# A hybrid decoder layer on one core: fifteen value, key and query units as three split products in the chunk loop

## The chip, the core and the metric

The kernel runs on one NeuronCore of a Trainium2 chip. Five engines take part: TensorE (PE, matrix products into eight PSUM banks), VectorE (DVE), ScalarE (ACT), GpSimd (POOL) and SyncE (SP, which issues most of the DMAs). Each runs its own instructions in order; semaphores order them against each other. The metric is the device time in microseconds of one execution.

## The reference, cut to what matters

One decoder layer for 256 prompt tokens and 8 sequences of 4 new tokens (288 token columns), D_MODEL 2048, everything in float32:

```
h = rmsnorm(x, g_mix)
proj = h @ w_in            # q, k, v (8 heads of 128 each), indexer q and k, gates, and the RWKV-7 inputs
o_a = sparse attention     # indexer scores, causal top-k, softmax over the selected keys;
                           # the 8 sequences also see 1024 cached keys each, by a page table
o_b, state = rwkv7(...)    # decay, delta-rule state of 16 heads of 64x64, per-head norm
mixed = sigmoid(ga) * (o_a @ w_pa) + sigmoid(gb) * (o_b @ w_pb)
x = x + mixed @ w_o
x = x + (silu(h2 @ w_gate) * (h2 @ w_up)) @ w_down      # h2 = rmsnorm(x, g_ffn)
y = rmsnorm(x, g_final)
```

The outputs also hold the rotated keys, the values, the indexer keys, the RWKV states and the last normalised rows.

## The kernel before, in words

**Units and tiles.** The weights of all projections come as units of 128 output columns: 16 blocks of 128x128 float32, 1 MB. SP loads unit u into slot u % 4 of `ring` once unit u - 4 has been read (`unit_read`), in the order of the program. A unit's result is a 128x288 tile that gathers in PSUM bank u % 2; ScalarE (or VectorE) copies it out and counts `bank_free`. The numbers U_SMALL to U_DOWN name where each kind of unit begins: U_IDX (27) to 30 are the indexer queries, U_VKQ (31) to 54 the 8 value, 8 key and 8 query units, U_GA (55) on the gates.

**Plain and split products.** In a plain unit each of 16 *tiles* is one float32 matmul of a weight block in `ring` with a 288-column block of `hT`, recorded as two instructions (`tile`, L472). In the first units and from the mixing on, the products are split: ScalarE copies weights and activations to a rounded format (fp32r, "high"), VectorE subtracts to get the "low" rest, and three products (high*high, low*high, high*low) stand for one float32 product (L504 to L506, L1032 to L1034, L1077 to L1079).

**Filling.** `fill` puts plain tiles into TensorE's program wherever other work leaves gaps. `vkq(t0, t1)` does it for value, key and query tiles counted from 32 on: `vkq(-32, ...)` starts with tile 0, so `vkq(6, 10)` is tiles 38 to 41. These places are written out by hand:

- The decay chain (about 195 to 285 us): the low-rank products (L585), then norms (L594, L602), bonus products (L617), nine gram products (L628, one for each chunk and one for the samples), with VectorE's long elementwise passes between. Here TensorE does the indexer units and the first value tiles.
- The sample part (285 to 364 us): self scores (L739), cached indexer scores (`scores`), the sample steps and the prompt's indexer scores. VectorE inverts the gram triangles (from L1793) and starts the top-k.
- The chunk loop (`chunk`, 364 to 563 us): 8 chunks of 32 tokens of the RWKV state. A chunk has four groups of small matmuls (transposes L794 and L796, x L812 and L816, u L825, outputs and state L834 to L842) with 6, 8, 7, 6 and 7 plain tiles ahead of, between and behind them: 34 tiles a chunk, 272 in all, after 112 that came earlier. ScalarE evicts after each group (`turned`: eight pieces behind the transposes) and stages the next chunk; VectorE evicts the other halves, multiplies the state, rotates the keys and queries that are complete (`rotate`) and goes on with the top-k (`largest`).
- Behind the loop: the value rows are turned (L854 to L860), then prompt attention and the cached scores (`kscore`, L929 to L939) alternate. Sequence 0's key pages (`first_keys`, 8 pages of 512 KB into KP[0]) are loaded during the loop. When `chunk_done` says that the loop is over and they have landed, SP reads the page numbers of sequence 1 (`keys_of`, L388) and issues its 16 half pages (`k_half`, L395).

**SP's order** around the gram stage: units up to U_VKQ + 3; then, after `dve_stage` 4, eight pages of indexer keys; for every chunk a gram store and one page; eight pages; unit U_VKQ + 4; eight pages; unit U_VKQ + 5; after `sidx`, sixteen pages; then the rest. GpSimd only issues DMAs between its first squares and the end.

`arena` is one SBUF area of 35520 columns whose parts serve several tensors in turn; `area(at, ...)` names a float32 view, `over(...)` one in fp32r.

Of the kernel before, what the change touches and what calls it, by code (L numbers as in the profile page):

```python
# [20 lines left out]
P = 128  # L21
# [26 lines left out]
U_DOWN = U_FF + 2 * FT  # L48
U_END = U_DOWN + 4 * KT

# [69 lines left out]
def program(nc, wst, wdn, xT, cst_d, prm_d, lora_d, kT_d, v_d, ki_d, wkv_d, pt_d, o_y, o_k, o_v, o_ki, o_wkv,  # L120
            o_shift, o_wkvs):
    with ExitStack() as ctx:
# [64 lines left out]
        UPD = [area(at, 2, NB * DB) for at in (9472, 15104, 1540, 28160)]  # L187
# [78 lines left out]
        def over(name, base, at, shape, dt=F32R):  # L266
# [15 lines left out]
                        over("first_h_lo", "arena", 7168 + KT * NX, [P, KT, NX]))  # L282
        x1_d = nc.dram_tensor("residual", (P, KT, NT), F32)
# [30 lines left out]
        def _(sp):  # L314
# [61 lines left out]
            units(U_VKQ + 5, U_VKQ + 6, unit)  # L376
# [21 lines left out]
            units(U_VKQ + 6, U_GA + 1, unit)  # L398
# [3 lines left out]
            first_keys(4, NPG)  # L402
# [9 lines left out]
            sp.wait_ge(sem("chunk_done"), NCH + 1)  # L412
            sp.wait_ge(sem("k_in0"), 16 * NPG)
# [42 lines left out]
        def _(pe):  # L456
# [132 lines left out]
            pe.wait_ge(sem("h_done"), 1)  # L589
            pe.wait_ge(sem("dve_stage"), 1)  # L590
            pe.wait_ge(sem("lora_out"), 2 * CT)
# [4 lines left out]
            fill(U_IDX, 6, 20)  # L596
# [7 lines left out]
            fill(U_IDX, 20, 42)  # L604
# [7 lines left out]
            for j in range(CT):  # L612
                if j == 4:
                    fill(U_IDX, 42, 4 * KT)
# [4 lines left out]
            vkq(-32, -17)  # L619
# [12 lines left out]

            vkq(-8, 2)
# [99 lines left out]
            vkq(2, 6)  # L733
# [8 lines left out]
            vkq(6, 10)  # L742
# [6 lines left out]
            vkq(10, 12)  # L749
            scores_sum(0)  # L750
            pe.wait_ge(sem("states_in"), 16)
            for j in range(CT):
                if j == 4:
                    sample_step(0)
                state_term(j)
                vkq(12 + 2 * j, 14 + 2 * j)
# [4 lines left out]
            vkq(28, 31)  # L761
            sample_step(1)
            vkq(31, 37)
            sample_step(2)
            for n in range(3, 7):
                vkq(25 + 4 * n, 29 + 4 * n)
# [5 lines left out]
            vkq(53, 58)  # L772
            sample_step(7)
            vkq(58, 62)
            sample_step(8)
            vkq(62, 66)
            sample_step(9)
            pe.wait_ge(sem("scs_out"), 2)
            for n in range(2 * IH):
                prompt_scores(n)  # L780
                if n % 2 == 1 and n < 14:
                    vkq(65 + n, 67 + n)
                if n == 5:
                    sample_step(10)
            at_tile = 112

            def chunk(n, at):

                fill(U_VKQ, at, at + 6)
# [9 lines left out]
                fill(U_VKQ, at + 6, at + 14)  # L799
# [19 lines left out]
                fill(U_VKQ, at + 14, at + 21)  # L819
# [8 lines left out]
                fill(U_VKQ, at + 21, at + 27)  # L828
# [16 lines left out]
                fill(U_VKQ, at + 27, at + 34)  # L845

            pe.wait_ge(sem("sample_act"), 63)
            for n in range(NCH):
                chunk(n, at_tile + 34 * n)
# [94 lines left out]
            for n in range(2 * HA + 3):  # L944
# [7 lines left out]
                if n == 7:  # L952
                    pe.wait_ge(sem("var_out"), CT)
                if n >= 7:
                    fill(U_GA, 11 * (n - 7), min(11 * (n - 6), 8 * KT))
# [182 lines left out]
        def _(act):  # L1138
# [75 lines left out]
            act.wait_ge(sem("index_rows"), 3)  # L1214
            ch(fn(SG, SG, ACT.Sigmoid))
# [4 lines left out]
            act.wait_ge(sem("lora_out"), 2 * CT)  # L1220
            act.wait_ge(sem("norm_out"), CT + 2)
# [25 lines left out]
            evict(-2 + 32)  # L1247
# [97 lines left out]
            evict(8 + 32)  # L1345
# [13 lines left out]
            evict(28 + 32)  # L1359
# [5 lines left out]
            evict(37 + 32)  # L1365
            sample_step(2)
            for n in range(3, 7):
                evict(29 + 4 * n + 32)
# [8 lines left out]
            evict(58 + 32)  # L1377
            sample_step(7)
            evict(62 + 32)
            sample_step(8)  # L1380
            evict(66 + 32)
            sample_step(9)
            for n in range(2 * IH):
                prompt_relu(n)
                evict(min(67 + n, 80) + 32)
                if n == 5:
                    sample_step(10)
            at_tile = 112
# [12 lines left out]
            def chunk(n, at):  # L1401
# [10 lines left out]
                evict(at + 14)  # L1412
                act.wait_ge(sem("x_done"), n + 1)
                fn(XS[0:CH], ps[2][0:CH, :].rearrange("p (h i) -> p h i", i=64), ACT.Copy).then_inc(sem("x_out"), 1)
                evict(at + 21)
# [4 lines left out]
                evict(at + 27)  # L1420
# [5 lines left out]
                evict(at + 34)  # L1426
# [4 lines left out]
            for n in range(NCH):  # L1431
                chunk(n, at_tile + 34 * n)
            act.wait_ge(sem("vrows"), 1)
            for t in range(2):
# [167 lines left out]
        def _(dve):  # L1602
# [273 lines left out]

            for n in range(NCH):
                chunk(n)
            rotate(HA - 1)
# [233 lines left out]
        def _(pool):  # L2113
# [30 lines left out]
            pool.wait_ge(sem("states_done"), 4)  # L2144
            pool.dma_start(o_wkvs, SST).then_inc(sem("wkvs_out"), 16)
# [101 lines left out]
```

## Time and profile before

| | us |
|---|---|
| median of 3 runs (range) | 1982.94 (1981.04 to 1983.49) |
| the profiled execution | 1981.97 |
| its span | 1979.7 |
| TensorE matmuls busy | 1938.5 (98%) |
| VectorE busy | 1024.7 (52%) |
| ScalarE busy | 729.1 (37%) |
| GpSimd busy | 38.2 (2%) |

The profile shows one execution. "Busy" leaves out waits, and matmuls overlap, so a busy TensorE need not be at its peak. In the lists below a group is: engine, line, operation, output <- input, count; times are in us from the start of the span. "Granted clock" (PEclk) is the share of TensorE's full clock that the chip allowed: 1.00 is 2.4 GHz, 0.50 is 1.2 GHz.

### The profile page before, as it was taken

To read this page: it belongs to the slowest core of one execution; us is meant where nothing else is said; L and a number is where in the kernel's file an instruction comes from. 1 tells how busy PE (TensorE), PEld (TensorE's weight loads), DVE (VectorE), ACT (ScalarE), POOL (GpSimd) and SP (SyncE) were. 2 spreads that over 40 slices of the span, in tenths; PEclk is the share of its full clock that TensorE was granted. 3 is DMA by queue.
4 is the path that set the end of the run, shared out by engine and by line. 5 is a ranking of instruction groups with operands and counts; after the bars stand their busy time and mean duration, and the time that the engine had idled before them with its cause. 6 is when DMAs were issued, how large, how long until landed. Compare 5 with 4: busy or idle time off the path is not lost.

```text
span 1979.7 us, 37998 instructions
## 1 busy us (share of the span) xinstructions
PE 1938.5 (98%) x15641; PEld 1769.2 (89%) x15641; DVE 1024.7 (52%) x1256; ACT 729.1 (37%) x963; POOL 38.2 (2%) x55
## 2 busy tenths in 40 slices
PE   8999999999989999999999999999999999999997
PEld 7999666688866766899999999999999999999997
DVE  6655849677644510455545545555544554444443
ACT  5333204422223110444444444444444444333332
POOL 0000011000000000000000000000000000000000
PEclk9999999999999999999999999999999999999999
DMA  6454284445567999544455544444444444544443
GB/s 262 167 174 170 99 239 130 138 131 189 186 250 265 345 380 403 201 164 170 170 209 183 192 168 160 163 168 170 169 160 162 166 170 150 209 161 162 168 166 121
DMA packets 105431, 376.35 MB, mean 190 GB/s; under 512 B 28898, under 2 KB 38754, under 8 KB 78210
## 3 DMA queue, kind: packets, MB, share of 16 engines
q1 hardware_dynamic: 78514, 344.13, 48.8%
q0 software_dynamic: 4576, 18.92, 2.8%
q10 hardware_dynamic: 22256, 12.13, 2.2%
q8 instruction: 58, 0.95, 0.2%
q14 instruction: 27, 0.22, 0.0%
HBM read 357.53 MB, written 17.58 MB: 189 GB/s over the span
## 4 chain that ended last, share of the span: by engine, by line
PE 93%; DVE 2%; SPq 2%; DMA 1%; ACT 1%; issue 1%; POOLq 0%; ACTq 0%; DVEq 0%
PE ps L472 16%; PE ps L1077 14%; PE ps L1078 14%; PE ps L1079 14%; PE ps L1032 5%; PE ps L1033 5%; PE ps L1034 5%; PE ps L505 3%; PE ps L504 3%; PE ps L506 3%; PE ps L988 1%; PE ps L939 1%; PE ps L516 1%; SPq L395 1%; DMA arena<-in_kT 1%
## 5 line engine op out<-in xcount | busy, mean ns | idle before, releaser
L2038 DVE TENSOR_TENSOR weights_lo<-ring,weights_hi 128x2048 fp32r<-128x2048 f32 (+1 forms) x152 | 305.7, 2011 | 284.9 <-ACT weights_hi L1546 284.9
L1078 PE MATMUL ps<-h_lo,weights_hi 128*128 128x288 f32 x1408 | 416.1, 296 | 0.0
L1077 PE MATMUL ps<-h_hi,weights_hi 128*128 128x288 f32 x1408 | 414.6, 294 | 0.4 <-DVE weights_lo L2038 0.4
L1079 PE MATMUL ps<-h_hi,weights_lo 128*128 128x288 f32 x1408 | 412.5, 293 | 0.0
L1546 ACT ACTIVATE weights_hi<-ring 128x2048 fp32r<-128x2048 f32 (+1 forms) x152 | 257.1, 1692 | 367.4 <-PE ps L1079 358.4
L472 PE MATMUL ps<-hT,ring 128*128 128x288 f32 x1408 | 368.4, 413 | 0.0
L472 PEld LDWEIGHTS ps<-hT,ring 128*128 128x128 f32 x1408 | 260.5, 191 | 77.8 <-issue 10.3
L1079 PEld LDWEIGHTS ps<-h_hi,weights_lo 128*128 128x128 f32 x1408 | 265.1, 188 | 0.0
L1077 PEld LDWEIGHTS ps<-h_hi,weights_hi 128*128 128x128 f32 x1408 | 264.1, 188 | 0.7 <-DVE weights_lo L2038 0.7
L1078 PEld LDWEIGHTS ps<-h_lo,weights_hi 128*128 128x128 f32 x1408 | 264.4, 188 | 0.1
L1077 PE MATMUL ps<-act_hi,weights_hi 128*128 128x288 f32 x704 | 208.4, 296 | 0.0
L1078 PE MATMUL ps<-act_lo,weights_hi 128*128 128x288 f32 x704 | 207.7, 295 | 0.0
L1079 PE MATMUL ps<-act_hi,weights_lo 128*128 128x288 f32 x704 | 207.0, 294 | 0.0
L1966 DVE TENSOR_TENSOR weights_lo<-ring,mix_weights_hi 128x2048 fp32r<-128x2048 f32 x48 | 110.0, 2292 | 90.2 <-ACT mix_weights_hi L1495 90.2
L1495 ACT ACTIVATE mix_weights_hi<-ring 128x2048 fp32r<-128x2048 f32 x48 | 91.8, 1913 | 119.0 <-PE ps L1034 119.0
L1079 PEld LDWEIGHTS ps<-act_hi,weights_lo 128*128 128x128 f32 x704 | 132.6, 188 | 0.0
L1078 PEld LDWEIGHTS ps<-act_lo,weights_hi 128*128 128x128 f32 x704 | 132.2, 188 | 0.0
L1077 PEld LDWEIGHTS ps<-act_hi,weights_hi 128*128 128x128 f32 x704 | 131.9, 187 | 0.0
L505 PE MATMUL ps<-first_h_lo,first_weights_hi 128*128 128x296 f32 x384 | 115.2, 300 | 0.0
L506 PE MATMUL ps<-first_h_hi,weights_lo 128*128 128x296 f32 x384 | 114.6, 299 | 0.0
L504 PE MATMUL ps<-first_h_hi,first_weights_hi 128*128 128x296 f32 x384 | 114.6, 298 | 0.0
L1145 ACT ACTIVATE first_weights_hi<-ring 128x2048 fp32r<-128x2048 f32 x27 | 51.7, 1915 | 93.7 <-PE ps L506 88.6
(369 smaller groups left out, 2876.4 us busy)
## 6 DMA issues: line engine op xcount, KB each, us to landing
ring<-in_wst SPq DMA_DIRECT2D x207, 1024.0 KB, 4.9
ring<-in_wdn SPq DMA_DIRECT2D x64, 704.0 KB, 4.0
arena<-in_v SPq DMA_DIRECT2D x64, 512.0 KB, 6.0
arena<-in_kT SPq DMA_DIRECT2D x112, 256.0 KB, 5.4
arena<-chunk_ar_bk ACTq DMA_DIRECT2D x24, 256.0 KB, 3.7
arena<-in_ki SPq DMA_DIRECT2D x64, 64.0 KB, 2.7
arena<-in_kT SPq DMA_DIRECT2D x8, 512.0 KB, 6.2
arena<-in_xT SPq DMA_DIRECT2D x4, 592.0 KB, 6.6
```

The costliest lines, as they stand in the source:

```text
L472: ins = mm(out, ring[:, slot, k, :], rhs(k), start=(k == 0), stop=(k == KT - 1))
L504: mm(out, W_HI1[:, (u0 + s) % 2, w], H_HI1[:, k, :], start=(k == 0), stop=False)
L505: mm(out, W_HI1[:, (u0 + s) % 2, w], H_LO1[:, k, :], start=False, stop=False)
L506: ins = mm(out, W_LO[:, slot, w], H_HI1[:, k, :], start=False, stop=(k == KT - 1))
L1032: mm(out, MW_HI[:, (u - U_MIX) % 2, w], hi, start=start, stop=False)
L1033: mm(out, MW_HI[:, (u - U_MIX) % 2, w], lo, start=False, stop=False)
L1077: mm(out, W_HI[:, (u - U_FF) % 2, w], hi, start=start, stop=False)
L1078: mm(out, W_HI[:, (u - U_FF) % 2, w], lo, start=False, stop=False)
L1079: return mm(out, W_LO[:, u % 4, w], hi, start=False, stop=stop)
L1546: fn(W_HI[:, (u - U_FF) % 2, 0:n], ring[:, u % 4].rearrange("p k c -> p (k c)")[:, 0:n], ACT.Copy).then_inc(sem("w_high"), 1)
L1966: tt(W_LO[:, u % 4], raw, MW_HI[:, (u - U_MIX) % 2].bitcast(F32), ALU.subtract).then_inc(sem("mix_w_split"), 1)
L2038: tt(W_LO[:, u % 4, 0:m], raw, W_HI[:, at, 0:m].bitcast(F32), ALU.subtract).then_inc(sem("w_split"), 1)
```

## The change

- 137 plain tiles now come before the loop instead of 112. The 25 more stand in the decay chain: `fill(U_IDX, 6, 10)` ahead of L594, 30 tiles instead of 22 ahead of L617, 19 instead of 15 ahead of the grams, two instead of one behind each gram. All later `vkq` calls are shifted by 25. In ScalarE's program the sigmoid of SG (L1215) moves behind the 16 low-rank sigmoids. SP loads unit U_VKQ + 6 ahead of the wait on `sidx`.
- Units U_VKQ + 9 to U_VKQ + 23 (15 units, the last seven key units and the eight queries) are done in the loop as split products: 720 of them, in halves of 24 (`key_products`), 94 a chunk (64 in chunk 0, 92 in chunk 7), divided over the five places of a chunk by `loop_part`. Seven plain tiles stand at the loop's start.
- ScalarE copies the high part of each half (1024 columns) into one of two buffers (`key_weights_high`), inside its chunk program at the places where it evicted units (`progress`), and before the loop the high part of h into four free pieces of SBUF.
- GpSimd subtracts the low part of each half in place in `ring`. The store of the sample states moves behind its 19th half.
- VectorE makes the low part of h in place of `hT` before the loop, and adds high and low again after it; TensorE's gate tiles wait for that.
- The free pieces lie where sequence 0's key pages 5 to 7 went: SP loads these only after the loop and after h is restored. UPD's second area moves.

```diff
+U_SPLIT, N_SPLIT = U_VKQ + 9, 15
+N_PLAIN = 137
+def loop_part(n, s):
+    part = lambda m: 0 if m < 0 else min(48 * N_SPLIT, (64 + 94 * (m // 5 - 1) + (17, 39, 58, 75, 94)[m % 5])
+                                          if m >= 5 else (0, 17, 33, 48, 64)[m])
+    return part(5 * n + s - 1), part(5 * n + s)
+def high_free(q):
+    return 0 if q < 2 else 24 if q == 2 else 24 * (q - 2) + 16
...
-            units(U_VKQ + 5, U_VKQ + 6, unit)
+            units(U_VKQ + 5, U_VKQ + 7, unit)
             sp.wait_ge(sem("sidx"), 1)
...
-            first_keys(4, NPG)
+            first_keys(4, 5)
...
             sp.wait_ge(sem("chunk_done"), NCH + 1)
+            sp.wait_ge(sem("first_h_split"), 5 * 4 + 8)
+            first_keys(5, NPG)
             sp.wait_ge(sem("k_in0"), 16 * NPG)
...
-            pe.wait_ge(sem("dve_stage"), 1)
             pe.wait_ge(sem("lora_out"), 2 * CT)
+            fill(U_IDX, 6, 10)
+            pe.wait_ge(sem("dve_stage"), 1)
...
-                vkq(-17 + c, -16 + c)
-            vkq(-8, 2)
+                vkq(-1 + 2 * c, 1 + 2 * c)
+            vkq(17, 27)
...
-            vkq(6, 10)
+            vkq(31, 35)
             scores(0)
...
+            def key_products(p0, p1):
+                for p in range(p0, p1):
+                    q, k, part = p // 24, p // 24 % 2 * 8 + p % 8, p % 24 // 8
+                    u = U_SPLIT + p // 48
+                    if p % 48 == 0:
+                        pe.wait_ge(sem("bank_free"), u + 1)
+                    kind = ("hh", "lh", "hl")[part] if q == 0 else ("hh", "hl", "lh")[part]
+                    if p % 24 == 0:
+                        pe.wait_ge(sem("first_high"), U_IDX + q + 1)
+                    if p == 0:
+                        pe.wait_ge(sem("first_h_high"), 5 * 4 + 4)
+                    if kind == "lh" and p % 8 == 0:
+                        pe.wait_ge(sem("first_split"), U_IDX + q + 1)
+                    if kind == "hl" and p < 48 and p % 8 == 0:
+                        pe.wait_ge(sem("first_h_split"), 5 * 4 + 4)
+                    ...
+                    if kind == "hl" and p % 8 == 7:
+                        ins.then_inc(sem("key_high_read"), 1)
...
+            def key_weights_high():
+                q = key_high[0]
+                u = U_SPLIT + q // 2
+                act.wait_ge(sem(f"w_in{u % 4}"), 16 * (u // 4 + 1))
+                if q >= 2:
+                    act.wait_ge(sem("key_high_read"), q - 1)
+                    act.wait_ge(sem("first_split"), U_IDX + q - 1)
+                fn(VW_HI[q % 2], ..., ACT.Copy).then_inc(sem("first_high"), 1)
+            def progress(to):
+                while key_high[0] < 2 * N_SPLIT and high_free(key_high[0]) <= to:
+                    if 48 * (evicted[0] - 8) <= high_free(key_high[0]):
+                        evict(KT * (evicted[0] + 1))
+                    else:
+                        key_weights_high()
+                while 48 * (evicted[0] - 8) <= to and evicted[0] < 3 * HA:
+                    evict(KT * (evicted[0] + 1))
+            act.wait_ge(sem("pidx_sum"), 2 * IH)
+            act.wait_ge(sem("wkv_out"), 16)
+            key_weights_high()
+            key_weights_high()
+            for a, b, high in V_HI:
+                fn(high[:, :, :], hT[:, a:b, 0:NT], ACT.Copy).then_inc(sem("first_h_high"), 1)
             act.wait_ge(sem("inv_stored"), 32 * NCH)
             stage_inverse(0)
             values(0)
...
+            dve.wait_ge(sem("unit_read"), U_SPLIT)
+            for g, (a, b, high) in enumerate(V_HI):
+                dve.wait_ge(sem("first_h_high"), 5 * 4 + g + 1)
+                tt(H_LO[:, a:b, 0:NT], hT[:, a:b, 0:NT], high[:, :, :].bitcast(F32), ALU.subtract)...
             for n in range(NCH):
                 chunk(n)
+            dve.wait_ge(sem("unit_read"), U_GA)
+            for a, b, high in V_HI:
+                tt(hT[:, a:b, 0:NT], H_LO[:, a:b, 0:NT].bitcast(F32), high[:, :, :].bitcast(F32), ALU.add)...
             rotate(HA - 1)
...
+            for q in range(2 * N_SPLIT):
+                u, at = U_SPLIT + q // 2, q % 2 * KT * P // 2
+                pool.wait_ge(sem("first_high"), U_IDX + q + 1)
+                nc.gpsimd.tensor_tensor(W_LO[:, u % 4, w], ring[...][:, w], VW_HI[q % 2].bitcast(F32),
+                                        ALU.subtract).then_inc(sem("first_split"), 1)
```

## Rows read from the trace of the kernel before

**Rows 1.** Windows: us, then busy us (count) of each engine, granted clock, DMA.

```profile
400.00:500.00 100.00, 100.00 (x1108) 80.64 (x1108) 77.54 (x116) 26.57 (x61) 0.60 (x1) 1.00 0.48 160
...
1300.00:1400.00 100.00, 100.00 (x760) 100.00 (x760) 50.60 (x48) 45.36 (x40) 0.00 (x0) 1.00 0.47 166
```

**Rows 2.** Table of waits, TensorE: us in total, times, longest.

```profile
PE ps L617 <- DVE arena L1713: 2.8, 1, 2.8
PE ps L628 <- DVE arena L1756: 2.2, 1, 2.2
```

**Rows 3.** Chain of waits, chunks 1 and 2: start, us, what.

```profile
410.45 6.50 PE ps L472 x26
...
435.27 6.50 PE ps L472 x26
```

**Rows 4.** Window of the decay chain behind the wait of L617.

```profile
232.00:236.00 4.00, 4.00 (x11) 2.79 (x10) 3.62 (x12) 0.00 (x0) 0.00 (x0) 0.57 0.00 0
```

**Rows 5.** Instructions in order of time, TensorE: start, us, instructions, [idle before <- releaser].

```profile
231.70 3.50 PE L617 MATMUL ps<-arena,cst 128*128 128x288 f32 x8 [2.80 <-DVE arena L1713]
...
246.10 2.10 PE L617 MATMUL ps<-arena,cst 128*128 128x288 f32 x8
```

**Rows 6.** Instructions in order of time, TensorE at the self scores.

```profile
285.10 0.42 PE L739 MATMUL ps<-arena 128*32 128x4 f32 x16 [0.82 <-ACT arena L1251]
```

**Rows 7.** Instructions in order of time, SP's queue behind the gram stores.

```profile
276.23 9.28 SPq L359 DMA_DIRECT2D arena<-in_ki  x9
285.55 0.44 SPq L316 DMA_DIRECT2D ring<-in_wst  x1
```

**Rows 8.** Line 316 between 284 and 287 us, issue to landing.

```profile
DMA to landing us min/median/max: 7.6/7.6/7.6
```

**Rows 9.** Instructions in order of time at the loop's entry, and wide passes.

```profile
212.29 2.12 ACT L1223 ACTIVATE arena<-arena 128x2304 f32<-128x2304 f32 x1
...
364.15 3.18 PE L472 MATMUL ps<-hT,ring 128*128 128x288 f32 x12
...
364.66 1.07 DVE L1787 SCALAR_TENSOR_TENSOR arena<-arena,small 128x256 f32<-128x256 f32 x2 [0.73 <-ACT arena L1245]
...
365.21 1.15 ACT L1318 ACTIVATE arena<-arena 128x512 f32<-128x512 f32 x2 [0.30 <-issue]
...
366.31 2.50 DVE L1844 TENSOR_TENSOR arena<-arena,prm 128x2304 f32<-128x2304 f32 x1
```

**Rows 10.** Instructions in order of time, ScalarE behind the transposes of chunk 2.

```profile
418.74 1.57 ACT L1397 ACTIVATE arena<-ps 32x256 f32<-32x256 f32 x4 [6.19 <-PE ps L796]
...
421.95 1.15 ACT L1318 ACTIVATE arena<-arena 128x512 f32<-128x512 f32 x2
```

**Rows 11.** Instructions in order of time, GpSimd and VectorE at the start.

```profile
5.29 4.17 POOL L2117 TENSOR_TENSOR arena<-arena 128x1152 f32<-128x1152 f32 x2 [4.83 <-DMA arena<-in_xT]
...
7.35 3.71 DVE L1632 SCALAR_TENSOR_TENSOR first_h_lo<-arena,prm,first_h_hi 128x288 fp32r<-128x288 f32 x4 [5.38 <-ACT first_h_hi L1154]
...
15.11 1.79 DVE L1632 SCALAR_TENSOR_TENSOR first_h_lo<-arena,prm,first_h_hi 128x288 fp32r<-128x288 f32 x4
```

**Rows 12.** Instructions in order of time, SP and TensorE around the loop's end.

```profile
528.13 3.62 SPq L383 DMA_DIRECT2D arena<-in_kT  x4
...
558.22 1.13 PE L842 MATMUL ps<-arena 64*64 64x64 f32 x32
...
562.78 1.04 PE L854 MATMUL ps<-cst,arena 128*128 128x128 f32 x8
...
564.15 12.14 SPq L395 DMA_DIRECT2D arena<-in_kT  x16
...
583.69 5.35 PE L939 MATMUL ps<-arena 128*32 128x256 f32 x64 [2.54 <-DMA arena<-in_kT]
```

**Rows 13.** Line 383 (key pages of 512 KB), issue to landing.

```profile
DMA to landing us min/median/max: 5.9/6.2/6.6
```

**Rows 14.** The page's GB/s of DMA in 40 slices of 49.5 us.

```profile
GB/s 262 167 174 170 99 239 130 138 131 189 186 250 265 345 380 403 201 164 170 170 209 183 192 168 160 163 168 170 169 160 162 166 170 150 209 161 162 168 166 121
```

More of the change, by code:

```diff
@@ L396, in k_half @@
                         "a p n -> p (a n)")[:, w]).then_inc(sem(f"k_in{half}"), 16)
-            units(U_VKQ + 6, U_GA + 1, unit)
+            units(U_VKQ + 7, U_GA + 1, unit)
             sp.wait_ge(sem("wkvs_out"), 16)
@@ L595, in _ @@
             ins.then_inc(sem("norm"), 1)
-            fill(U_IDX, 6, 20)
+            fill(U_IDX, 10, 24)
             pe.wait_ge(sem("norm_out"), CT + 3)
@@ L603, in _ @@
                    tile_position=(g, 0)).then_inc(sem("norm"), 1)
-            fill(U_IDX, 20, 42)
+            fill(U_IDX, 24, 54)
             def vkq(t0, t1):
@@ L613, in _ @@
                 if j == 4:
-                    fill(U_IDX, 42, 4 * KT)
+                    fill(U_IDX, 54, 4 * KT)
+                    vkq(-32, -20)
                 if j >= 4:
@@ L781, in _, with chunk @@
                 if n % 2 == 1 and n < 14:
-                    vkq(65 + n, 67 + n)
+                    vkq(90 + n, 92 + n)
                 if n == 5:
                     sample_step(10)
-            at_tile = 112
-            def chunk(n, at):
-                fill(U_VKQ, at, at + 6)
+            def key_products(p0, p1):
[13 more added lines that the diff above has]
+                        pe.wait_ge(sem("first_h_split"), 5 * 4 + 4)
+                    k0, high = [(a, t) for a, b, t in V_HI if a <= k < b][0]
+                    w = (W_LO[:, u % 4, k * P:(k + 1) * P] if kind == "lh" else VW_HI[q % 2][:, k % 8 * P:(k % 8 + 1) * P])
+                    h = H_LO[:, k, 0:NT] if kind == "hl" else high[:, k - k0, :]
+                    ins = mm(ps[u % 2][:, 0:NT], w, h, start=(p % 48 == 0), stop=(p % 48 == 47))
+                    if kind == "hl" and p % 8 == 7:
+                        ins.then_inc(sem("key_high_read"), 1)
+                    if p % 48 == 47:
+                        ins.then_inc(sem("unit_read"), 1)
+            def chunk(n):
+                if n == 0:
+                    fill(U_VKQ, N_PLAIN, 9 * KT)
+                key_products(*loop_part(n, 0))
                 pe.wait_ge(sem("sbk_in"), 32 * (n + 1))
@@ L798, in chunk @@
                 ins.then_inc(sem("turned"), 1)
-                fill(U_VKQ, at + 6, at + 14)
+                key_products(*loop_part(n, 1))
                 pe.wait_ge(sem("sgr_in"), 16 * (n + 1))
@@ L818, in chunk @@
                 ins.then_inc(sem("x_done"), 1)
-                fill(U_VKQ, at + 14, at + 21)
+                key_products(*loop_part(n, 2))
                 pe.wait_ge(sem("sti_in"), 32 * (n + 1))
@@ L827, in chunk @@
                 ins.then_inc(sem("u_done"), 1)
-                fill(U_VKQ, at + 21, at + 27)
+                key_products(*loop_part(n, 3))
                 pe.wait_ge(sem("u_out"), 2 * n + 2)
@@ L844, in chunk @@
                 ins.then_inc(sem("chunk_done"), 1)
-                fill(U_VKQ, at + 27, at + 34)
+                key_products(*loop_part(n, 4))
             pe.wait_ge(sem("sample_act"), 63)
             for n in range(NCH):
-                chunk(n, at_tile + 34 * n)
+                chunk(n)
             pe.wait_ge(sem("state"), NCH + 1)
@@ L1399, in turned, with chunk @@
                        ACT.Copy).then_inc(sem("turned_out"), 1)
-            def chunk(n, at):
+            def chunk(n):
                 if n == 1:
```

81 lines of the change are left out of this document (50 added, 31 removed).

## The prediction

> **What bounds the kernel now.** I read the windows of 100 us first: between 400 and 500 us, inside the chunk loop, TensorE is busy all the time while VectorE stands at 77.5 and ScalarE at 26.6 us [rows 1]. The table of waits then shows that TensorE idles in few places: in the decay chain (2.8 us ahead of the blk products of L617, 2.2 us ahead of the gram products of L628) [rows 2]. So little is lost anywhere else: a plain tile taken out of the loop is worth its full time, and a tile put into the decay chain costs only what the idle time there does not swallow. Last I read the queues and the other engines in order of time around four places: the gram stage, the loop's entry, the inside of a chunk, the loop's end. The change adds a wait or moves a transfer at each of them.
>
> The sum is made against the profiled execution's own 1981.97 us (span 1979.7); the median of the runs is 1982.94, 1.0 us more. A measurement here can tell about 0.2%, 4.0 us, from no change.
>
> **1. Split products for plain tiles (gain).** The 13 plain tiles between two chunks' matmuls, recorded as 26, take 6.50 us, and a chunk lasts 24.8 us [rows 3]; a tile is 0.500 us and a chunk's 34 tiles are 17.0. A split product of the same shape runs in the FFN at 760 per 100 us [rows 1], 0.132 us. Chunks 1 to 6 each issue 94 of them (12.4 us), chunk 7 issues 92 (12.1), chunk 0 issues 7 plain tiles and 64 products (11.9). That is 6 x 4.6 + 4.9 + 5.1 = 37.8 us less. The 7.8 us of scan matmuls per chunk stay.
>
> **2. 25 tiles into the decay chain.** They are 12.5 us of work: 4 ahead of the norms, 8 ahead of L617, 4 ahead of the grams, 9 among them. They replace the 2.8 and 2.2 us of idle time and some 4 us of shorter waits. Behind the 2.8 us the granted clock was 0.57 on average, with 1.2 GHz in part of the stretch [rows 4], and the same eight products took 3.50 us instead of 2.10 [rows 5]; a long wait costs some 1.7 us beyond itself, and two such are covered here. VectorE's chain starts 1.2 us later because four tiles now stand ahead of the norm matmuls; moving the SG sigmoid gives 0.7 back. Followed wait by wait, the self scores (L739, at 285.10) [rows 6] come 0.8 us later: **+0.8**, between -1 and +3.
>
> **3. Unit 35 is wanted before it is loaded.** PE now does tile 64 of the value and key units (the first of unit U_VKQ + 4) right behind L739; before, it was at tile 38 there. SP loads that unit in an unchanged place: behind the last gram store and nine index-key pages that take 9.28 us, so at 285.55, and it landed 7.6 us later [rows 7, 8]. The grams' end moves it by 0.5 us, to a landing at 293.6. PE comes from L739 at 286.3, does one tile and waits from 286.8: 6.8 us, and 1.7 for the clock, **+8.5** (5 to 9: less if it lands sooner or the clock stays up). Behind PE wait the cached scores and, through ScalarE's in-order queue, the odd gram loads of VectorE's inverse, so nothing downstream takes it back.
>
> **4. Entry of the loop.** TensorE's last prompt score before the fill ended at 364.15 [rows 9]. It then does 7 plain tiles, 3.5 us, to 367.7, and needs `sv_done` for the transposes (chunk 0 has no split product ahead of them). ScalarE must first wait for VectorE's last prompt sum (365.7), then copy two halves of weights and the whole of h, 6656 columns. By 2.12 us for 2304 columns that is 6.6 us with the fixed parts of six instructions, to 372.4; then two DMA issues and the value copies (1.15 us) end at 374.5 [rows 9]. Idle time 6.8 us, +1.7 clock: **+8.5** (6 to 10). GpSimd's two low halves and VectorE's low part of h (5.4 us) end before product 16 needs them.
>
> **5. High parts inside a chunk.** ScalarE makes the high part of half q only after product 24q - 32, and stands in its own order: after the transposes it evicts for 3.2 us and copies values for 1.15 [rows 10], then copies the half (1.0 us), 5.4 us after the transposes. Half 8 (freed at product 160, two products into chunk 2) is wanted at product 192, 17 products or 2.2 us behind the transposes; half 12 in chunk 3 after 19, half 16 in chunk 4 after 21. TensorE waits 3.2, 3.0 and 2.7 us, each with 1.7 of clock: **+14.0** (9 to 16; below, if the clock stays up). The other halves are freed early enough.
>
> **6. Evictions against a shorter part.** The x matmuls need ScalarE's evictions, 3.2 us after the transposes [rows 10]. The 8 tiles between hid them; 17 products (2.2 us) in chunk 0 and 22 (2.9 us) later don't: 1.1 + 4 x 0.4 = **+2.7** (chunks 2 to 4 are already waiting).
>
> **7. GpSimd's subtraction.** The trace has GpSimd on 1152 columns in 2.1 us [rows 11], none with this output. For 1024 columns I take 1.9 to 2.3; below is no gain, since only a late one is seen. A half is consumed every 5 us, so up to 3.5 us costs at most 1.5, and 4.2 us (twice the row) 6. I take 0.
>
> **8. Behind the loop.** VectorE restores h in four passes, 5.4 us by 2.50 for 2304 columns [rows 9], ahead of the last rotation. SP loads pages 5 to 7 only then: issues 0.9 us apart (3.62 for four), landing in 6.2 [rows 12, 13], so the last is in 14.0 us after the last value, key and query product. Only then does SP read the next page numbers (4.8 us: from the last chunk's end at 559.3 to the first issue at 564.15) and start sequence 1's 16 half loads. Before, these started 1.4 us after that product (564.15 against 562.8), and the matmuls on them at 583.69 [rows 12], 20.9 us after it. Now: 14.0 + 4.8 + 3.5 MB ahead of the first half's end and 1 MB of g2, 4.5 MB at the 403 GB/s of the densest slice [rows 14], 11.2, + 2 to land = 32.0. **+11.2** (7 to 15); both versions have the slow clock there. The extra idle time of sequence 0's scores lies inside it.
>
> Sum: -37.8 + 0.8 + 8.5 + 8.5 + 14.0 + 2.7 + 0 + 11.2 = **+7.9 us**: 1989.9 on the profiled basis, 1991 on the runs' median.
>
> **The shared port, by row and by page.** While GpSimd squared x (5.29 to 9.46), four scaled subtractions of VectorE took 3.71 us instead of 1.79 [rows 11]: VectorE stood still, GpSimd did not slow. The Trainium skill ("SBUF — State Buffer", "Who interferes with whom") says that a VectorE instruction with two SBUF inputs and a GpSimd instruction that reads SBUF exclude each other for the whole instruction; the trace agrees. By that rule each of the 30 low halves can hold VectorE or be held: where no such meeting lies on the path the sum stays 1991, with one in each chunk it is the last rival's time.
>
> **Rivals.**
> - *Not the forecast's stalls but ScalarE in time* (faster). If the copies of halves 8, 12 and 16 end within 2.2 us of the transposes, step 5 is gone: 1991 - 14 = 1977. For it: ScalarE is busy only 26.6% [rows 1]. Against: what counts is its order, and 4.35 us of other work stands ahead. Chance 0.17.
> - *The load of unit 35 hides* (no change): 1991 - 8.5 = 1982.5. It decides at a landing before 287. For it: only the queue's order makes it late. Against: DMA queues were full then. 0.18.
> - *The key pages hide*: if the loads behind the loop overlap what PE waits for anyway, step 8 falls by 11 to 1980. Against: sequence 1's scores already waited 2.5 us before the change [rows 12]. 0.10.
> - *VectorE becomes the bound.* Its work in a chunk is 0.775 x 24.8 = 19.2 us on average [rows 1, 3], against 20.2 for TensorE's new chunk. One block of 2.1 us per chunk on the path makes 7 x 2.1 = 15 us: 2006. It decides once VectorE loses over 1 us a chunk. Against: the waits of steps 5 and 6 give it room. 0.08.
> - The forecast, all steps within their bounds, 1984 to 1999: 0.47.
>
> The range takes in the bounds of the steps and reaches to the first rival: 1977 to 1999. Slower by over 0.2% (above 1986.9): most of the forecast, the fourth rival and a little of the second, 0.57. Within 0.2%: the second and third mostly, 0.25. Faster (below 1979): 0.18.
>
> **What would show it.** Step 1: the loop's products at 0.132 us each. Step 2: no wait over 1 us before L739. Step 3: TensorE idle some 7 us behind L739, ended by a DMA into ring. Step 4: 7 us idle ahead of the first transposes, ended by ScalarE. Step 5: three waits near 3 us on ScalarE's high parts in chunks 2, 3 and 4, none in 5 to 7. Step 8: sequence 1's scores 32 us after the last query product. Wrong would be: a chunk near 20.5 us throughout, or waits on GpSimd's low parts in most chunks.

## The result, and the profile after

The changed kernel takes 2005.18 us (median of 4 runs, 2000.17 to 2008.33) against 1981.99 us before: ratio 1.0114, 95% interval 1.0091 to 1.0136, so 23.2 us slower. The forecast was 1991 (1977 to 1999): the sign came out, the size was about three times too small (+7.9 us in the sum), and the time lies outside the range. The profiled run took 2005.82 us, with a span of 2004.0: 24.3 us more than before.

TensorE's table of waits in the changed kernel (us in total, times, longest):

```profile
PE ps L988 <- DMA arena<-in_kT: 11.8, 3, 6.9
PE ps L828 <- ACT key_weights_hi_a L1449: 8.9, 3, 3.2
...
PE ps L493 <- DMA ring<-in_wst: 6.6, 1, 6.6
PE ps L919 <- DVE arena L1913: 5.7, 1, 5.7
PE ps L843 <- ACT arena L1369: 5.4, 1, 5.4
PE ps L861 <- ACT arena L1477: 3.0, 5, 0.8
```

The waits of [rows 2] are gone, and those of steps 3, 4, 5, 6 and 8 stand in their place. In order of time on TensorE and SyncE's queue (start, us, instructions, idle time before):

```profile
285.48 0.42 PE L762 MATMUL ps<-arena 128*32 128x4 f32 x16 [0.30 <-ACT arena L1302]
293.20 3.25 PE L493 MATMUL ps<-hT,ring 128*128 128x288 f32 x6 [6.62 <-DMA ring<-in_wst]
...
374.04 3.66 PE L493 MATMUL ps<-hT,ring 128*128 128x288 f32 x14
383.07 1.94 PE L843 MATMUL ps<-cst,arena 128*128 128x128 f32 x8 [5.37 <-ACT arena L1369]
...
428.48 1.23 PE L828 MATMUL ps<-h_lo,key_weights_hi_b 128*128 128x288 f32 x8
429.54 0.43 PE L828 MATMUL ps<-key_h_hi_b,weights_lo 128*128 128x288 f32 x2
...
433.99 0.64 PE L828 MATMUL ps<-key_h_hi_a,key_weights_hi_a 128*128 128x288 f32 x3 [3.24 <-ACT key_weights_hi_a L1449]
...
569.56 1.03 PE L903 MATMUL ps<-cst,arena 128*128 128x128 f32 x8
575.72 2.51 SPq L402 DMA_DIRECT2D arena<-in_kT  x3
586.60 6.53 PE L988 MATMUL ps<-arena 128*32 128x256 f32 x64 [4.63 <-DMA arena<-in_kT]
591.13 9.55 SPq L414 DMA_DIRECT2D arena<-in_kT  x16
608.06 6.04 PE L988 MATMUL ps<-arena 128*32 128x256 f32 x64 [6.95 <-DMA arena<-in_kT]
```

The self scores (285.10 in [rows 6]) start at 285.48. The fill ahead of the loop (364.15 in [rows 9]) starts at 374.04, 9.9 us later. The loop, from that fill to the value rows' transposes (562.78 in [rows 12], 569.56 here), takes 195.5 us instead of 198.6. From there to sequence 1's scores it is 38.5 us instead of 20.9: +17.6. What comes later is as long as before (1395.94 and 1396.01 us). So 9.9 - 3.1 + 17.6 - 0.1 = 24.3 us: all of the loss has a place.

Windows of the same run; the last column but two is the granted clock. The first row is chunk 2, the second chunk 5, the third lies behind the loop; the last is the kernel before, behind its loop:

```profile
426.59:453.92 27.33, 24.09 (x305) 22.89 (x303) 19.83 (x31) 10.56 (x19) 9.70 (x4) 0.88 0.36 116
507.73:529.26 21.53, 20.97 (x304) 20.00 (x303) 17.49 (x25) 10.35 (x19) 9.78 (x5) 1.00 0.53 168
...
576.00:590.00 14.00, 6.79 (x58) 3.20 (x62) 4.23 (x10) 0.83 (x3) 0.00 (x0) 0.50 0.57 198
```
```profile
564.00:582.00 18.00, 13.96 (x151) 9.00 (x148) 11.02 (x28) 5.69 (x16) 1.61 (x3) 1.00 0.91 337
```

A chunk with no wait but one of 0.56 us lasts 21.4 to 21.5 us, down from 24.8 [rows 3]. A chunk with a 3.24 us wait lasts 27.3, and the clock was at 1.2 instead of 2.4 GHz in a quarter of it. Behind the loop it was at 1.2 GHz throughout 576 to 590. In the kernel before it was not: 1.00 from 564 to 582, and 0.72 in the 6 us after that.

### The profile page after: what moved, and what is told of

Read it like the earlier page. It is cut to its first block, busy times and chain, and to the rows that moved or that the text cites. A ratio compares the mean times of both kernels' runs of the same rounds, so it can differ in the third digit from the quotient of the medians.

```text
span 2004.0 us, 38581 instructions
## 1 busy us (share of the span) xinstructions
PE 1933.3 (96%) x15881; PEld 1786.5 (89%) x15881; DVE 1049.1 (52%) x1264; ACT 763.0 (38%) x997; POOL 112.9 (6%) x85
## 4 chain that ended last, share of the span: by engine, by line
PE 91%; ACT 2%; DMA 2%; SPq 2%; DVE 1%; issue 1%; ACTq 0%; DVEq 0%
PE ps L1128 14%; PE ps L1129 14%; PE ps L1130 14%; PE ps L493 10%; PE ps L1083 5%; PE ps L1085 5%; PE ps L1084 5%; PE ps L828 4%; PE ps L526 3%; PE ps L525 3%; PE ps L527 3%; PE ps L1039 1%; DMA arena<-in_kT 1%; PE ps L988 1%; PE ps L537 1%
## 5 line engine op out<-in xcount | busy, mean ns | idle before, releaser
L493 PE MATMUL ps<-hT,ring 128*128 128x288 f32 x928 | 246.0, 416 | 8.0 <-DMA ring<-in_wst 6.6
L493 PEld LDWEIGHTS ps<-hT,ring 128*128 128x128 f32 x928 | 172.6, 192 | 62.6 <-issue 11.8
```

Of the source, the lines that this page charges most:

```text
L493: ins = mm(out, ring[:, slot, k, :], rhs(k), start=(k == 0), stop=(k == KT - 1))
```

## The experiments

My theory was that the loss is a sum of separate waits, each with a stretch of lower clock behind it. The main rival was the prediction's last: GpSimd's subtractions hold VectorE on the shared port, and VectorE becomes the bound of the loop. Medians below stand against the changed kernel's 2005.2 us, which was timed on its own; the ratios are to the kernel before, timed on the same chip beside each experiment (1980.5 to 1982.1 us), so a difference of 2 us between medians says nothing.

**e1_load**: unit 35's load ahead of eight key pages.

```
+            units(U_VKQ + 4, U_VKQ + 5, unit)
             ki_pages(2, 0, 8)
-            units(U_VKQ + 4, U_VKQ + 5, unit)
```

> The changed kernel (2005.2 us) with one edit on SyncE: the load of unit U_VKQ + 4 is issued ahead of the eight index-key pages of pair 2 instead of behind them. Theory (the loss is a sum of added waits, each with a stretch of lower clock behind it): the 6.6 us wait of the plain tiles at 293 us goes, and with it the 10.2 us at the lower clock that cost some 2.9; the loop's fill starts at 364.5 instead of 374.0 and the time is 1996, between 1994 and 1998. Rival (the waits in front of the loop are not what sets the end: VectorE's inverse and the gram loads would have held the loop back anyway): the wait goes, another ahead of the loop takes its place, and the time stays above 2003.

Measured: 2002.6 us (1997.5 to 2007.6), ratio 1.0091 [1.0057, 1.0125]. A miss: the time fell between the theory's and the rival's. The load was issued at 274.81 instead of 285.46, but TensorE still waited 5.2 us for it. Its one landing time, and what the DMA engines did meanwhile (second last column their busy share, last column GB/s; the next experiment's expectation says 120 GB/s, these rows say 350 and 203):

```profile
DMA to landing us min/median/max: 14.8/14.8/14.8
```
```profile
276.00:282.00 6.00, 6.00 (x28) 4.53 (x27) 5.90 (x4) 0.00 (x0) 5.30 (x8) 1.00 1.02 350
282.00:288.00 6.00, 2.14 (x23) 1.14 (x21) 0.87 (x3) 2.44 (x7) 0.57 (x1) 0.93 0.98 203
```

SyncE's order is only a part of what makes the load late: the DMA engines are full from 276 to 288 us, and the load issued into them took 14.8 us to land. What it gained was lost again behind it. TensorE went on 3.55 us earlier than in the changed kernel (289.65 against 293.20) and was 3.5 us later at 352.60 (349.07). Between them ScalarE's seven gram loads took 9.00 us to issue instead of 4.59, its next eviction came late, and TensorE waited and then had the lower clock. The first row is the changed kernel's, the others are e1_load's:

```profile
299.55 4.59 ACTq L1403 DMA_DIRECT2D arena<-gram  x7
```
```profile
295.52 9.00 ACTq L1403 DMA_DIRECT2D arena<-gram  x7
308.31 1.92 PE L687 MATMUL ps<-arena,small 64*32 64x512 f32 x4 [1.57 <-ACT arena L1391]
```
```profile
308.00:320.00 12.00, 11.69 (x84) 7.68 (x84) 10.74 (x36) 1.77 (x5) 0.00 (x0) 0.50 0.59 186
```

This is the rival's picture, in one profiled run, the second slowest of six.

**e1b_load**: the same load ahead of the gram stores (`units(U_VKQ + 4, U_VKQ + 5, unit)` above `for c in range(NCH):`).

> In e1_load the load was issued 10.7 us earlier (274.8 instead of 285.5) and landed only some 3.5 us earlier, 14.9 us after its issue, beside the gram stores' short packets (DMA engines busy all the time at 120 GB/s). Here the load of unit U_VKQ + 4 is issued ahead of the first gram store, near 263. Theory (what made unit 35 late is the DMA engines' queue in the gram stage, of which the issue's place is only a part): it lands before 283, no wait over 0.5 us for the ring before 300, no lower clock at 289, and the fill ahead of the loop starts 8 to 10 us earlier than in the changed kernel (374.0); time 1996, between 1992 and 1999. Rival (the data behind the grams, index keys and gram loads, are late themselves): the 5 to 7 us of idle time appear at the cached scores or the states instead, and the time stays above 2001.

Measured: 2000.6 us (1998.5 to 2003.8), 1.0093 [1.0069, 1.0118]. The wait for the ring is gone, and another stands at the grams: VectorE waits for a gram store behind the MB, and TensorE for VectorE. The time fell by 4.6 us and lies between the theory's range and the rival's mark, as in e1_load.

```profile
263.76 0.44 SPq L335 DMA_DIRECT2D ring<-in_wst  x1
270.59 1.51 DVE L1837 TENSOR_TENSOR arena<-ps,cst 128x512 f32<-128x512 f32 x2 [8.91 <-DMA gram<-arena]
271.34 1.97 PE L651 MATMUL ps<-arena 64*64 64x64 f32 x32 [4.73 <-DVE arena L1837]
```

**e7_load_first**: the load earlier still, behind unit 34 and ahead of SyncE's wait for the B and K rows (`units(22, U_VKQ + 5, unit)`).

> The changed kernel with the load of unit U_VKQ + 4 issued ahead of SyncE's wait for the B and K rows, so ahead of the index-key pages of pair 1 too, near 250 us, when its slot of the ring is free. e1_load and e1b_load turned the wait of 6.6 us into waits of 5.2 us for the same load and of 4.7 us for the gram stage. Theory (from 253 us the DMA engines are full, and a MB put in anywhere among them is paid for by someone; before that they have room): no wait over 1 us for the ring or for the gram stage, the fill ahead of the loop starts at 365 instead of 374, time 1996, between 1993 and 1999. Rival (the engines have no room at 250 either): another wait of 4 us or more between 250 and 300, time above 2000.

Measured: 1991.9 us (1989.1 to 1995.8), 1.0042 [1.0018, 1.0066]: 13.3 us less, more than expected (1993 to 1999). Issued at 248.15 it landed in 4.8 us, in a place where the changed kernel's DMA engines are busy only a quarter of the time (this row is the changed kernel's), and no wait replaced it (rows of e7_load_first):

```profile
250.00:254.00 4.00, 4.00 (x18) 3.13 (x17) 3.73 (x10) 0.40 (x1) 0.77 (x1) 1.00 0.26 100
```
```profile
283.73 0.42 PE L761 MATMUL ps<-arena 128*32 128x4 f32 x16 [0.34 <-ACT arena L1301]
284.08 2.21 PE L492 MATMUL ps<-hT,ring 128*128 128x288 f32 x8
```

The first transposes of the loop start at 371.79. In the changed kernel they start at 383.07, and in e2_high, e3_keys, e5_zero_low and e10_tail, whose programs are the same up to there, at 380.87 to 383.86. So the load was worth 9.1 to 12.1 us there, and some 2 us of the gain can be the spread between runs.

**e2_high**: ScalarE copies freed high halves before it waits for the transposes.

```
+                progress(loop_part(n, 0)[1])
                 act.wait_ge(sem("turned"), n + 1)
```

> The changed kernel with one line more on ScalarE: in each chunk the high halves that the products ahead of the transposes have freed are copied before ScalarE waits for the transposes. Theory (waits and the clock behind them): the three waits on high halves (3.2, 3.0, 2.7 us) fall below 0.5 us each, the three stretches of 6.8 us at the lower clock in chunks 2, 3 and 4 go too (3.4 us each), and the time falls by 17 to 19 us to 1987, between 1984 and 1990. Rival (VectorE, held by GpSimd's subtractions on the port that both use, is the bound of a chunk): the three waits turn into waits on VectorE's copies or state, and the time stays above 2002.

Measured: 1992.7 us (1990.7 to 1998.8), 1.0046 [1.0024, 1.0068]: -12.5 us, short of 17 to 19 and outside the range (1984 to 1990). The three waits are gone. Chunks 2 and 4 of e2_high, and the long wait left in chunk 4:

```profile
427.08:448.48 21.40, 20.84 (x304) 19.97 (x303) 19.82 (x30) 10.56 (x19) 10.11 (x5) 1.00 0.47 159
469.90:494.91 25.01, 22.44 (x305) 21.45 (x304) 24.29 (x33) 10.34 (x19) 10.96 (x5) 0.93 0.62 211
```
```profile
482.10 1.39 PE L874 MATMUL ps<-arena 32*32 32x64 f32 x32 [2.00 <-DVE arena L1936]
```

Chunks 2 and 3 fell from 27.3 and 27.1 to 21.4 us; in chunk 4 (26.7 before) VectorE, busy 24.3 of 25.0 us, now comes last at the u matmuls, 2.0 us plus the clock. It is late because it meets GpSimd twice just before, in the two instructions of its last update of the sample states (rows of e2_high):

```profile
467.50 3.42 DVE L1920 TENSOR_TENSOR arena<-arena 128x1024 f32<-128x1024 f32 x1
470.95 3.29 DVE L1921 TENSOR_TENSOR arena<-arena,small 128x1024 f32<-128x1024 f32 x1
```
```profile
467.23 2.60 POOL L2239 TENSOR_TENSOR weights_lo<-ring,key_weights_hi_b 128x1024 fp32r<-128x1024 f32 x1 [5.74 <-ACT key_weights_hi_b L1449]
469.82 3.33 POOL L2239 TENSOR_TENSOR weights_lo<-ring,key_weights_hi_a 128x1024 fp32r<-128x1024 f32 x1
```

The same two VectorE instructions take 1.22 and 1.23 us in the update before (446.10), which begins between two subtractions (GpSimd's next one starts at 448.14), and 1.22 each in e5_zero_low, where GpSimd reads nothing: 4.3 us less for the pair. So the rival has its place, but in one chunk of eight, and there it costs 3.6 us (25.01 against 21.40). That the 2.0 us wait would go with GpSimd's reads is inferred; no run took them out of e2_high.

**e5_zero_low**: GpSimd writes zeros and reads nothing (`nc.gpsimd.memset(W_LO..., 0.0)`), so the weights' low parts are left out.

> The changed kernel with GpSimd writing zeros instead of the low parts of the 15 split units: the weights' low parts are left out of the result; GpSimd no longer reads SBUF for them, every signal and every product stays. Theory (waits on ScalarE and SyncE, with the clock): none of the waits goes, VectorE's instructions in the loop get shorter (no L1961 of 3.1 us, no L1951 of 2.1 us), and the time falls by 0 to 2 us: 2004, between 2002 and 2006. Rival (the shared port makes VectorE the bound of the loop): the loop gets at least 1 us a chunk shorter, 1996 or less.

Measured: 2002.6 us (1996.8 to 2006.2), 1.0091 [1.0056, 1.0126]. Two undisturbed chunks of the changed kernel, and then two of e5_zero_low:

```profile
507.73:550.66 42.93, 41.82 (x606) 39.97 (x605) 37.54 (x52) 20.66 (x38) 19.25 (x9) 1.00 0.63 208
```
```profile
502.27:545.13 42.86, 41.74 (x607) 39.99 (x606) 34.90 (x55) 20.65 (x38) 7.62 (x8) 1.00 0.62 201
```

VectorE's busy time falls by 2.6 us and GpSimd's by 11.6, the two chunks' by 0.07. The rival falls for the undisturbed chunks, and for those alone; chunk 4 of e2_high is the other case. The 2.6 us between the medians is inside the spread of both.

**e3_keys**: behind the loop, sequence 0's pages on a semaphore of their own; no wait for their landing.

```
             sp.wait_ge(sem("chunk_done"), NCH + 1)
+            pages = keys_of(1)
             sp.wait_ge(sem("first_h_split"), 5 * 4 + 8)
             first_keys(5, NPG)
-            sp.wait_ge(sem("k_in0"), 16 * NPG)
-            pages = keys_of(1)
```

> The changed kernel with SyncE's order behind the loop changed: sequence 0's pages count on a semaphore of their own, sequence 1's page numbers are read before SyncE waits for the restored h, and its half loads follow the last three pages of sequence 0 at once, without waiting for their landing. Theory (the exposed part of step 8 is SyncE's in-order chain: wait for landing, read numbers, issue): sequence 1's first half load is issued 12 us earlier, near 579 instead of 591.1, its scores start 8 to 12 us earlier than 608.1, and the time is 1995, between 1992 and 1998. Rival (behind the loop the DMA queues are the bound, or VectorE's restore and rotation are): the loads are issued earlier but the scores start within 3 us of 608, and the time stays above 2002.

Measured: 1993.8 us (1988.0 to 1996.1), 1.0048 [1.0028, 1.0068]: -11.4 us, as expected. SyncE's chain was the exposed part, and sequence 1's scores (last row) no longer wait:

```profile
573.09 2.51 SPq L402 DMA_DIRECT2D arena<-in_kT  x3
575.79 15.50 SPq L414 DMA_DIRECT2D arena<-in_kT  x16
582.90 6.30 PE L986 MATMUL ps<-arena 128*32 128x256 f32 x64 [3.49 <-DMA arena<-in_kT]
...
597.02 3.62 PE L986 MATMUL ps<-arena 128*32 128x256 f32 x61
```

The number is in part luck. The profiled run is 12.1 us shorter than the changed kernel's: 8.5 us between the last product and sequence 1's scores (30.0 us instead of 38.5), 1.0 later, and 2.6 ahead of the loop's end, where the edit changes nothing but chunks 2 and 4 happened to lose less to the clock (25.76 and 25.25 us instead of 27.33 and 26.75).

**e10_tail**: e3_keys, and VectorE rotates after its second pass over h, SyncE issues page 5 behind the last product, 6 and 7 behind that pass.

> e3_keys with two more edits behind the loop: VectorE rotates the last keys and queries after the second of its four passes over h, and SyncE issues page 5 of sequence 0 right behind the last product and pages 6 and 7 behind that second pass. Theory (behind the loop it is VectorE's and SyncE's order, not the amount of data, that holds TensorE): the wait of the second prompt score falls from 5.7 to about 3.6 us, sequence 0's scores start 2 to 3 us earlier than in e3_keys, time 1991, between 1988 and 1994. Rival (the data's arrival is the bound): 1993 or more.

Measured: 1992.7 us (1987.9 to 1995.1), 1.0046 [1.0025, 1.0066]. The rotation's wait fell from 5.7 to 3.7 us and sequence 0's scores start 12.1 us behind the transposes of the value rows instead of 15.9, and sequence 1's 27.4 us behind them instead of 30.0. But the median is only 1.1 us lower than e3_keys, less than either's spread: the trace shows the shorter stretch, the time does not decide. (In its profiled run chunks 2 and 4 lost 3 us more to the clock than in e3_keys.)

**e4_entry**: ScalarE loads the inverse and copies chunk 0's values ahead of the high parts.

> The changed kernel with ScalarE's order at the loop's entry changed: the inverse's loads and the copies of chunk 0's values come ahead of the high parts of the first two halves and of h. Theory (what TensorE waits for at the entry is ScalarE's work as a whole, 6.6 us of high parts and 1.15 us of values, all of it wanted before product 0): the wait ahead of the transposes falls below 2 us, but one of 3 to 6 us appears ahead of the first split products; time 2003, between 2001 and 2006. Rival (only what stands ahead of the transposes counts): 5.4 us and the clock are gained, 1997.

Measured: 2004.8 us (1998.7 to 2011.2), 1.0111 [1.0054, 1.0167]. The 5.37 us wait split in two, 3.06 + 2.18:

```profile
381.15 0.63 PE L828 MATMUL ps<-key_h_hi_a,key_weights_hi_a 128*128 128x288 f32 x3 [3.06 <-ACT key_h_hi_d L1471]
...
386.81 0.40 PE L828 MATMUL ps<-h_lo,key_weights_hi_a 128*128 128x288 f32 x1 [2.18 <-DVE h_lo L1961]
```

The entry is work, not order, as the theory had it.

**e8_entry_tiles**: 7 plain tiles taken from between the prompt scores to the entry (`N_PLAIN = 130`, `vkq(91 + n // 2, 92 + n // 2)`).

> The changed kernel with one plain tile instead of two behind each second prompt score (7 tiles, 3.5 us), and these 7 tiles at the loop's entry, ahead of the first transposes. e4_entry showed that ScalarE's order does not shorten the entry. Theory (it is 5.4 us of ScalarE's work that only other matmuls can cover): the wait at the entry falls to 2 us, its lower clock goes, time 2001, between 1998 and 2003. Rival (the tiles between the prompt scores cover waits for ScalarE's and VectorE's sums): the 3.5 us come back there as waits, time above 2003.5.

Measured: 1999.9 us (1996.8 to 2003.0), 1.0085 [1.0052, 1.0118]: -5.3 us, the wait 1.97 us as forecast.

**e0_tiles**: the kernel before with the 25 moved tiles alone.

```
-            at_tile = 112          (34 tiles a chunk)
+            at_tile = 137          (31 tiles a chunk: 5, 8, 6, 6, 6)
```

> The kernel before with the 25 moved weight tiles alone (with their load order and the sigmoid behind the lora): no split products, the loop keeps 247 plain tiles, 31 a chunk (5, 8, 6, 6, 6). Theory: the loop starts 9.9 us later than before (wait for unit 35 and its clock) and is 12.5 us shorter; time 1979.5, between 1977 and 1983, with a wait of 6 to 7 us for the ring near 293 and none at the entry over 1 us. Rival (the tiles of the loop cover waits, and a chunk with 31 is no shorter): 1985 or more.

Measured: 1979.9 us (1977.7 to 1983.9), 0.9985 [0.9965, 1.0005]: on the theory's number. The move by itself is worth nothing: what the loop gains, the wait for unit 35 takes (first line). A chunk of 31 tiles lasts 23.36 us, from the transposes of chunk 1 to those of chunk 2, instead of 24.82:

```profile
PE ps L472 <- DMA ring<-in_wst: 6.5, 1, 6.5
```
```profile
402.79 1.04 PE L797 MATMUL ps<-cst,arena 128*128 128x128 f32 x8
...
426.15 1.04 PE L797 MATMUL ps<-cst,arena 128*128 128x128 f32 x8
```

**e6_all**: e1b_load, e2_high, e3_keys and e4_entry together.

> The changed kernel with e1b_load, e2_high, e3_keys and e4_entry together. Theory (the losses are separate waits and add up): -9 for the load, -12.5 as e2_high gave, -11.4 as e3_keys gave, -2 for the entry: 1970, between 1965 and 1976, below the kernel before (1982). Rival (each removed wait moves into the next): 1980 or more.

Measured: 1981.2 us (1979.4 to 1982.2), 0.9987 [0.9964, 1.0010]. Their single gains (4.6 + 12.5 + 11.4 + 0.4) give 1976.3: 5 us are missing. This misses the theory's range (1965 to 1976) and meets the rival's mark (1980 or more): the parts do not simply add up, and 24 of their 29 us were kept. Its table of waits has the gram wait (5.1 us), VectorE's 2.0 us of e2_high, and VectorE's low part of h at the entry grown to 3.3 us.

**e9_best**: e2_high, e7_load_first, e8_entry_tiles and e10_tail, with shorter first parts of the chunks (`(14, 40, 58, 75, 94)` for `(17, 39, 58, 75, 94)`), so that more products lie above ScalarE's evictions.

> The changed kernel with e2_high, e7_load_first, e8_entry_tiles and e10_tail together, and 14, 26, 18, 17, 19 products in the parts of a chunk instead of 17, 22, 19, 17, 19 (chunk 0: 24, 14, 13, 13). Theory (separate waits, which add up where none of them moves into another): -9 (the load), -4 (the entry), -12.5 (the high parts), -14 (behind the loop), from 2005: 1966, between 1961 and 1972, at least 0.5% below the kernel before. Rival (as in e6_all, whose parts added up to 1976 and which took 1981, a good part of each moves on): 1974 or more.

Measured: 1962.7 us (1960.1 to 1965.4), 0.9903 [0.9875, 0.9931]: 19 us faster than the kernel before. The single gains (12.5 + 13.3 + 5.3 + 12.5 = 43.6) give 1961.6. That this fits so well is luck: the fifth edit, the shorter parts, had no run of its own, and an undisturbed chunk lasts 20.9 us here instead of 21.4, so the four others gave some 4 to 5 us less than their sum. The largest loss left is chunk 4, 26.43 us with the meeting of VectorE and GpSimd seen in e2_high. What it still waits for, without the waits at the start of the program:

```profile
PE ps L919 <- DVE arena L1913: 3.7, 1, 3.7
...
PE ps L987 <- DMA arena<-in_kT: 2.8, 2, 1.9
PE ps L874 <- DVE arena L1935: 2.5, 1, 2.5
PE ps L843 <- ACT arena L1368: 2.0, 1, 2.0
```

## Why the prediction was wrong, step by step

Every wait of the forecast stood in the trace at its place; three terms were mis-sized, all the same way. In the profiled run:

| step | forecast | measured | how |
|---|---|---|---|
| 1 split products | -37.8 | -32.6 | the loop's -3.1 without the loop's waits and clock below |
| 2 tiles moved | +0.8 | +0.4 | 285.48 - 285.10 |
| 3 unit 35 | +8.5 | +9.5 | 9.9 - 0.4 |
| 4 entry | +8.5 | +7.9 | 5.37, and about 2.5 for slow transposes and products |
| 5 high halves | +14.0 | +18.6 | chunks of 27.3, 27.1, 26.7 us less 3 x 20.84 |
| 6 evictions | +2.7 | +3.0 | five waits |
| 7 GpSimd | 0 | 0 | e5_zero_low, within its spread |
| 8 behind the loop | +11.2 | +17.6 | 38.5 - 20.9 |

They add up to +24.4, against 24.3 of the span. Step 1 is what is left of the loop's -3.1 when steps 4, 5 and 6 are taken out, so the sum proves nothing about it. Step 2's +0.4 is within the spread: the runs with the same program up to there reach the self scores between 283.5 and 285.8.

**Step 8 failed most (6.4 us).** The parts were named and two of the three were short. The last value, key and query product to the first of pages 5 to 7: 6.2 us. From there to the scores that need them 10.9 us: the three issues take 2.5 and TensorE's wait ends 8.4 us behind the last of them, where I took 6.2 from [rows 13]. The page numbers took 4.5 (4.8 forecast). From SyncE's first half load to the scores it took 16.9 us instead of 13.2: I had priced it at the 403 GB/s of the densest slice, though the same 16 loads took 19.5 us in the kernel before (564.15 to 583.69 in [rows 12]). What slowed them against 403 GB/s no run separates. I also wrote that both versions have the slow clock there. Only the new one has it, ahead of the scores; but both waits on the chain (4.63 and 6.95 us) end with a DMA, so this does not explain the 6.4 us. The chain itself was right: e3_keys cut it, and the stretch became 8.5 us shorter.

**Step 1 (5.2 us).** 0.132 us per product holds inside a run of products (8 in 1.06 us, 428.48 to 429.54), but a chunk without clock loss lasts 21.40 us. Without its 0.56 us wait and the 7.8 us of scan matmuls that is 13.04 us for 94 products, 0.139 each. The 0.132 is not what failed. The last chunk, which has 19 products fewer behind its first transposes, is 2.50 us shorter than the one before (18.90 and 21.40): 0.132 each. The mistake is the plain tile. I took 0.500 us from a run of 13 tiles that includes the change to the next group; in e0_tiles three tiles fewer made a chunk 24.82 - 23.36 = 1.46 us shorter, 0.487 each. (The kernel before has its transposes at 391.98 and 416.79.) By that 34 tiles were 16.55 us instead of 17.0 and the rest of a chunk 8.27 instead of 7.8, which is 0.45 of the 0.6 us a chunk. The other 0.2 us stay open.

**Step 5, its clock term (4.6 us).** The waits came out at 3.24, 2.98 and 2.71 us (3.2, 3.0, 2.7 forecast). The 1.7 us for the clock did not: chunk 2 took 27.33 us, of which 20.84 + 3.24 are work and wait, so 3.25 us is the clock's. In e1_load the same chunk with the same wait took 25.74, so 1.67:

```profile
429.83:455.57 25.74, 22.51 (x304) 21.28 (x303) 19.82 (x30) 10.56 (x19) 9.73 (x4) 0.93 0.38 125
```

A granted clock of 0.93 over 25.74 us is 3.6 us at 1.2 GHz, and 0.88 over 27.33 is 6.6: the same wait costs one price or twice that. I had the price from a single wait [rows 4, 5], which happened to be the lower one. It is the rarer one: nine profiled runs have the three waits, and of these 27 chunks 20 paid the higher price and 7 the lower (chunk 3 the higher one always). Why it is now one and now the other, no run shows. The changed kernel's four runs fit this: a mean granted clock of 0.986 in the one of 2000.17 us, 0.981 or 0.982 in those of 2004.5 to 2008.3.

**Steps 3, 4, 6.** Within a microsecond, for step 3 by a margin smaller than the spread between runs. Step 3's number was right and its mechanism half right: I named SyncE's order, and e1_load, e1b_load and e7_load_first show that it is order and full DMA engines together. The second rival ("only the queue's order makes it late") would have failed for the same reason.

**Step 7 and the shared port.** No TensorE wait on a low part is in the table, so the 0 was right, though an undisturbed subtraction took 2.4 us, above the 1.9 to 2.3 assumed. VectorE was held, but off the path. By the Trainium skill ("SBUF — State Buffer", "Who interferes with whom") the shared port pair is an exclusive lock, and the trace agrees: in the rows of e2_high above VectorE and GpSimd take turns, VectorE's 1.22 us instruction ends at 470.92, 1.1 us after GpSimd's first subtraction, and GpSimd's second, begun at 469.82, takes 3.33 us instead of 2.4. So GpSimd is held too, which the prediction had not seen at the start of the program. The price is 0.07 us in two undisturbed chunks (e5_zero_low), and a 2.0 us wait with its clock in chunk 4 once the wait of step 5 no longer covers it.

**The range.** It took each step's bounds one at a time, and gave step 1 none. Steps 5 and 8 fell outside theirs (9 to 16 and 7 to 15 us, against 18.6 and 17.6). That all the long waits of one run can pay the higher clock price, so that they go wrong together, was not in it.

## What to carry to other kernels

When a change makes the covering work cheaper, list what each piece of it covered; here the 32.6 us gained in the loop met waits at five places, and the gain only showed (1962.7 us) once each had other cover or was issued elsewhere. A transfer that comes late is not mended by issuing it a little earlier among others: look in the windows for a stretch where the DMA engines have room and issue it there. Take the time of a group of transfers from the same group in the trace before, not from the best rate seen. Price a TensorE wait by its whole chunk, wait plus what the clock takes behind it, and take that from several occurrences, not from one.

## What the hardware showed that I had not expected

The lower clock behind waits of the same length (3.23 and 3.24 us) lasted 3.6 us in one run and 6.6 in another. A 1 MB load landed in 4.8, 7.7 or 14.8 us, when issued at 248, 285 or 275 us: issued 10.7 us earlier into full DMA engines, it was there only 3.6 us earlier. Two VectorE instructions of 1.22 us and two GpSimd subtractions of 2.4 us, issued against each other, took 3.42, 3.29, 2.60 and 3.33 us. GpSimd's memset of 1024 columns took 0.95 us.
